# A hybrid layer with a mixture of experts and a two-layer decoder on one core: 36 instead of 40 tokens in the second set of gathered rows, eight row dots moved ahead, and the first loads in quarters

## What is computed

```python
    def per_chunk(args):
        xc, ec, gc = args
        u = expert_u[ec]
        a = jnp.einsum('cd,chkd->chk', xc, u).astype(jnp.float32)
        w = (jax.nn.gelu(a) * gc).astype(xc.dtype)
        return jnp.einsum('chk,chkd->cd', w, expert_v[ec])
```

## Time and profile before

| | |
|---|---|
| median of 3 runs | 1807.74 us (1807.58 to 1809.18) |
| the profiled execution | 1809.13 us |
| its span in the trace | 1807.3 us |
| mean granted clock of TensorE | 0.988 |
| PE busy | 1750.7 us, 97% of the span |
| DVE busy | 1071.6 us, 59% |
| moved by DMA | 439.59 MB |

### The profile page before, as it was taken

The page is one execution under the profiler, slowest core; times in us unless marked ns, Lnnn a source line. Parts: engine busy times, 40 slices in busy tenths (PEclk is TensorE's granted clock), DMA queues, the critical chain, the costliest instruction groups (busy, mean ns, idle before and its releaser), DMA issues.

```text
span 1807.3 us, 29102 instructions
## 1 busy us (share of the span) xinstructions
PE 1750.7 (97%) x11633; PEld 1491.7 (83%) x11633; DVE 1071.6 (59%) x2312; ACT 252.3 (14%) x598; POOL 292.4 (16%) x282
## 2 busy tenths in 40 slices
PE   8999999999999999999999499999999999999996
PEld 7888566986999999999999367699955978699942
DVE  2851432589855886998433743259974223369964
ACT  1004530111443111000000011111100001111100
POOL 0010000033333342444332500000000000000000
PEclk9999999999999999999999699999999999999998
DMA  7535224378999999999999953364554434354551
GB/s 278 190 138 165 93 94 140 125 280 296 418 417 415 408 387 383 364 414 415 416 418 417 373 211 121 131 238 164 167 184 163 162 118 168 126 173 166 173 175 47
DMA packets 76463, 439.59 MB, mean 243 GB/s; under 512 B 8562, under 2 KB 8640, under 8 KB 37568
## 3 DMA queue, kind: packets, MB, share of 16 engines
q1 hardware_dynamic: 42336, 304.11, 45.6%
q0 software_dynamic: 32592, 126.44, 18.1%
q10 hardware_dynamic: 1424, 7.47, 1.0%
HBM read 432.67 MB, written 5.24 MB: 242 GB/s over the span
## 4 chain that ended last, share of the span: by engine, by line
PE 86%; DMA 8%; DVE 3%; issue 1%; ACT 1%; POOL 0%; DVEq 0%; POOLq 0%; ACTq 0%
PE ps L864 15%; PE ps L1104 12%; PE ps L498 10%; PE ps L540 9%; PE ps L456 9%; PE ps L872 6%; DMA arena<-v_rows,sparse_pairs 6%; PE ps L1125 4%; PE ps L578 3%; DMA arena<-u_rows,sparse_pairs 2%; PE ps L732 2%; PE ps L779 2%; PE ps L842 2%; PE ps L745 1%; DVE arena L1945 1%; PE ps L959 1%
## 5 line engine op out<-in xcount | busy, mean ns | idle before, releaser
L872 PE MATMUL ps<-arena,ring 128*128 128x152 f32 (+1 forms) x2048 | 269.7, 293 | 0.4 <-DMA ring<-stream 0.4
L864 PE MATMUL ps<-xT,ring 128*128 128x152 f32 x2048 | 269.7, 293 | 0.0
L872 PEld LDWEIGHTS ps<-arena,ring 128*128 128x128 f32 x2048 | 265.5, 190 | 1.1 <-issue 1.1
L864 PEld LDWEIGHTS ps<-xT,ring 128*128 128x128 f32 x2048 | 265.7, 190 | 0.5 <-issue 0.5
L498 PE MATMUL ps<-ring,arena 128*128 128x512 f32 x416 | 181.4, 592 | 0.4 <-ACT arena L1406 0.4
L1945 DVE SCALAR_TENSOR_TENSOR arena<-arena,sparse_dots 128x1024 f32<-128x1024 f32 x105 | 134.7, 1283 | 76.1 <-DMA arena<-v_rows,sparse_pairs 70.5
L540 PEld LDWEIGHTS ps<-xT,ring 128*128 128x128 f32 x1536 | 173.4, 192 | 3.0 <-issue 2.9
L540 PE MATMUL ps<-xT,ring 128*128 128x128 f32 x1536 | 174.1, 275 | 0.0
L1831 DVE CUSTOM_DVE_ANT_0 arena<-arena 128x1024 f32<-128x1024 f32 x107 | 128.2, 1222 | 68.8 <-DMA arena<-u_rows,sparse_pairs 68.2
L2371 POOL DMA_INDIRECT arena<-u_rows,sparse_pairs x107 | 126.0, 1177 | 213.4 <-DVE sparse_dots L1831 183.6
L2371 POOL DMA_INDIRECT arena<-v_rows,sparse_pairs x107 | 129.5, 1211 | 185.0 <-DVE arena L1945 123.8
(11 more groups left out here) (329 smaller groups left out, 2162.1 us busy)
## 6 DMA issues: line engine op xcount, KB each, us to landing
ring<-stream SPq DMA_DIRECT2D x288, 1024.0 KB, 6.7
arena<-second_params POOLq DMA_DIRECT2D x6, 1024.0 KB, 5.5
arena<-kv_scratch POOLq DMA_DIRECT2D x2, 2048.0 KB, 14.3
kv_scratch<-arena POOLq DMA_DIRECT2D x2, 1024.0 KB, 6.6
kv_scratch<-arena ACTq DMA_DIRECT2D x2, 1024.0 KB, 10.7
arena<-held_params ACTq DMA_DIRECT2D x1, 2048.0 KB, 16.5
arena<-u_rows,sparse_pairs POOLq DMA_INDIRECT x107, 13.1
arena<-v_rows,sparse_pairs POOLq DMA_INDIRECT x107, 13.7
```

The lines of the kernel that those rows point to most:

```text
L864: ins = pe.matmul(ps[:, o % 2, 0:DENSE], w[:, (o % 2) * D + k * P:(o % 2) * D + (k + 1) * P], xT[:, k, 0:DENSE], start=(k == 0), stop=(k = ...
L872: ins = pe.matmul(ps[:, 4 + k // 2, c:c + DENSE], w[:, (o % 2) * D + k * P:(o % 2) * D + (k + 1) * P], H[:, n, :], start=False, stop=last, ...
```

## The change

The second set of tokens by rows has 36 instead of 40 tokens, so 100 of 256 go by rows and `DENSE` is 156. The dense tokens then make 20 gate groups of 8, of which the last has 4 tokens. `DOTS_HEAD` goes from 2 to 4, `DOTS_ROUTING` from 38 to 46, `DOTS_FIRST` from 56 to 60. `SETS_B`, `PAIRS_B`, `CHUNKS`, `U_FIRST`, `ROWS` and the 48 adds of the second mixed stage stay. Both first loads are issued as four quarters instead of two halves.

```diff
-SPARSE_B = 40
+SPARSE_B = 36
 SETS_B = P // SPARSE_B
 SPARSE = SPARSE_A + SPARSE_B
 DENSE = T - SPARSE
 GROUP = 8
-GROUPS = DENSE // GROUP
+GROUPS = -(-DENSE // GROUP)
 PAIRS_HALF = 64
 PAIRS_B = -(-P // SETS_B)
 CHUNKS = PAIRS_HALF + PAIRS_B
 PH_LATE = 4
-DOTS_HEAD = 2
+DOTS_HEAD = 4
 DOTS_EARLY = DOTS_HEAD * PH_LATE
-DOTS_ROUTING = 38
-DOTS_FIRST = 56
+DOTS_ROUTING = 46
+DOTS_FIRST = 60
...
-            half = SLOT // 2
-            sp.dma_start(ring[:, 0, 0:half], streams[0][0][:, 0:half]).then_inc(first_half_in, 16)
-            sp.dma_start(ring[:, 0, half:], streams[0][0][:, half:]).then_inc(loaded[0], 16)
+            quarter = SLOT // 4
+            for n in range(3):
+                c = slice(quarter * n, quarter * (n + 1))
+                sp.dma_start(ring[:, 0, c], streams[0][0][:, c]).then_inc(first_quarter_in[n], 16)
+            sp.dma_start(ring[:, 0, 3 * quarter:], streams[0][0][:, 3 * quarter:]).then_inc(loaded[0], 16)
...
-            pe.wait_ge(first_half_in, 16)
-            pe.wait_ge(mem_half_in, 16)
             for k in range(KT):
-                if k == KT // 2:
+                if k == 6:
                     pe.wait_ge(mem_in, 16)
                     slot("k0", 0)
+                elif k % 2 == 0:
+                    pe.wait_ge(first_quarter_in[k // 2], 16)
+                    pe.wait_ge(mem_quarter_in[k // 2], 16)
...
-            half = KT * T // 2
-            act.dma_start(mem_raw[:, 0:half], mem_d[:, 0:half]).then_inc(mem_half_in, 16)
-            act.dma_start(mem_raw[:, half:], mem_d[:, half:]).then_inc(mem_in, 16)
+            quarter = KT * T // 4
+            for n in range(3):
+                c = slice(quarter * n, quarter * (n + 1))
+                act.dma_start(mem_raw[:, c], mem_d[:, c]).then_inc(mem_quarter_in[n], 16)
+            act.dma_start(mem_raw[:, 3 * quarter:], mem_d[:, 3 * quarter:]).then_inc(mem_in, 16)
...
-                w = min(P, DENSE - i * P)
+                w = min(P, GROUPS * GROUP - i * P)
...
-                h = H[:, hf * HALF_BLOCKS:(hf + 1) * HALF_BLOCKS, g * GROUP:(g + 1) * GROUP]
-                dve.scalar_tensor_tensor(h, h, 1.0 / GSCALE, ps[:, 2 + b, :].rearrange("p (t n) -> p n t", t=GROUP),
+                n = min(GROUP, DENSE - g * GROUP)
+                h = H[:, hf * HALF_BLOCKS:(hf + 1) * HALF_BLOCKS, g * GROUP:g * GROUP + n]
+                dve.scalar_tensor_tensor(h, h, 1.0 / GSCALE, ps[:, 2 + b, :].rearrange("p (t n) -> p n t", t=GROUP)[:, :, 0:n],
                                          ALU.mult, ALU.mult).then_inc(gates_applied, 1)
```

More of the change, by code:

```diff
@@ L173, in build @@
         mark_cell = sb("mark_cell", [P, 1])
-        sel16 = sb("sel16", [P, 4, DENSE], F16)
+        sel16 = sb("sel16", [P, 4, GROUPS * GROUP], F16)
         e1 = sb("e1", [P, 2, 2, GROUP, HEAD], F16)
@@ L387, in build @@
         xkv_ready, xq_ready = sem("xkv_ready"), sem("xq_ready")
-        first_half_in, mem_half_in = sem("first_half_in"), sem("mem_half_in")
+        first_quarter_in = [sem(f"first_quarter_in_{n}") for n in range(3)]
+        mem_quarter_in = [sem(f"mem_quarter_in_{n}") for n in range(3)]
         mem_in, kv_spilled, kv_in = sem("mem_in"), sem("kv_spilled"), sem("kv_in")
```

## The result

| | before | after |
|---|---|---|
| median of 7 runs | 1808.11 us (1807.00 to 1809.18) | 1813.24 us (1812.62 to 1814.09) |
| ratio, 95% interval | | 1.003 (1.0021 to 1.0039) |
| the profiled execution, its span | 1809.13, 1807.3 us | 1812.62, 1810.8 us |

The change costs 5.1 us, where +5.4 us was forecast.

A forecast was written before the change was run, and what follows sets the result against it. PE's passes set the time, except one wait for the row path, bound after 740 us by DMA bytes shared with the stream. +6.9 - 1.5 = +5.4 us on 1807.74 gave 1813.1 us; range over the cases 1809.5 to 1817.0.

The forecast's parts named there:

- The tokens, +6.9: End of the row path: add 91 comes +6.6 us later, or +7.3 reckoned by bytes; +6.9 taken.
- The start of the second mixed stage: DVE's L1986 waits for ACT's gelu after PE's last up-block, so it moves with PE's passes: +7.3 us.
- PE's last wait: PE's wait at L959 for the row path shrinks from 24 to about 16 us and stays.
- ten less 5.8 gathers: Last row adds: 7.3 us more of full rate before the stream stops fetches 5.8 gathers earlier, 8.0 us.
- 0 to 1.3 us: Second mixed stage: gathers may fall behind the DMA engines by at most one gather, 1.3 us; 0 taken.
- The second rival: Row path: gathers stay at 3.2 us each while the stream runs; +9.9 us, 1817.6 us; chance 0.10.
- The early dots, 0: Eight dots moved into tile 1's routing: DVE about 11 us later there, hidden by waits; the lead is lost later.
- a net lead of four gathers: First mixed stage: eight dots ahead, four more to do; some 13 us less waiting, DVE done near 558 us.
- the cover: DVE's slack before the gates, done near 558 us, needed at 574.76 plus 3.4; without it PE waits microsecond for microsecond.
- The first rival: End of the row path: the eight-gather lead lives on to add 91, 11 us off, about 1802 us; chance 0.05.
- The first loads, -1.5: PE's start: the first quarter lands near 5.4 us instead of 6.95, gain kept; bounds 0 and -3.1 us.
- the 1.6 us added behind the bytes: First loads: delay from bytes moved to the landing PE saw, added to 3.85 us for a quarter.

The follow-up runs named there:

- e2: Kernel before with only 36 instead of 40 tokens in set B (20 gate groups), loads in halves, dots not moved; 1815.41 us, ratio 1.0043.
- e3: Kernel before with only the dots moved ahead (4 per head, 46, 60), 40 tokens, loads in halves; 1809.11 us, ratio 1.0006.
- e7: Kernel of e3 with ACT's exponentials of tile 0's gates after 28 instead of 24 up-blocks; 1808.02 us, ratio 1.0001 to the kernel before.
- e8: Changed kernel with four PE matmuls on a zero tile ahead of the first loads' wait; 1813.52 us, ratio 1.0032 to the kernel before.
- e5: Changed kernel with `U_FIRST` 103 instead of 96, seven more dots ahead of the v rows; 1803.18 us, ratio 0.9974 to the kernel before.
- e1: Kernel before with only the first loads in quarters instead of halves; 1805.78 us, ratio 0.9988.
- e6: Kernel of e5 with 42 tokens in set B, `U_FIRST` 107 and exponentials after 28 up-blocks; 1787.78 us, ratio 0.989 to the kernel before.
- e4: Kernel before with 42 instead of 40 tokens in set B (150 dense columns); 1806.60 us, ratio 0.999.

## Why the prediction was right

**The tokens, +6.9.** Measured alone +7.5 (e2; interval 5.2 to 10.1). The steps: a pass of 156 columns was put at 129.3 + 3.3 = 132.6 ns and took 132.5. The start of the second mixed stage was put 7.3 us later through PE's passes; U to M grew by 7.15 us in both kernels with 36 tokens. PE's last wait was put at 16 us and was 17.4 (17.1 in e2). Fewer than ten adds back to back were forecast, ten less 5.8 gathers or about four, and there were six. PE's work from its first up-block to its last wait grew by 13.9 us, where 14.6 was put, and PE's start behind that wait came 588.38 us after the first up-block instead of 580.94, +7.4 us (e2: +7.1). One reading would explain two more adds: the last stage moved 412 GB/s and not 416, 4 GB/s less over 264 us, 1.06 MB, two gathers. That is an account from two windows, not an experiment; if it holds, the 0 taken out of "0 to 1.3 us" for the gathers falling behind was too low.

**The rates add up.** The first and the last dot of the eleven late u rows, before and after, stood at

```profile
906.08 1.23 DVE L1831 CUSTOM_DVE_ANT_0 arena<-arena 128x1024 f32<-128x1024 f32 x1 [2.20 <-DMA arena<-u_rows,sparse_pairs]
...
938.46 1.23 DVE L1831 CUSTOM_DVE_ANT_0 arena<-arena 128x1024 f32<-128x1024 f32 x1 [2.21 <-DMA arena<-u_rows,sparse_pairs]
```

```profile
907.18 1.23 DVE L1837 CUSTOM_DVE_ANT_0 arena<-arena 128x1024 f32<-128x1024 f32 x1 [1.55 <-DMA arena<-u_rows,sparse_pairs]
...
938.29 1.23 DVE L1837 CUSTOM_DVE_ANT_0 arena<-arena 128x1024 f32<-128x1024 f32 x1 [1.60 <-DMA arena<-u_rows,sparse_pairs]
```

Ten intervals in each: 3.24 us a gather before, 3.11 after. A slot of the stream is 32 passes, 4.14 us before and 4.24 after, or 253 and 247 GB/s; what is left of 416, the rate from 880 to 935 us in both traces, is 163 and 169, 3.22 and 3.10 us for 0.524 MB. So the gathers do get what the slower stream leaves. The second rival, with gathers that keep their 3.2 us, has fallen, and its +9.9 us lies outside the measured interval (3.8 to 7.1). The trace agrees with the rule of the Trainium skill (DMA: Bandwidth & Descriptors, SWDGE vs HWDGE vs iDMA) named there, by which each engine takes its queues in turn; it does not show how the engines choose.

**The early dots, 0.** The end was right: U to M of the changed kernel equals e2's, and e3 shows no gain. The steps to it were not. DVE was to be done near 558 us, 13 us sooner, by a net lead of four gathers; measured were 565.5 instead of 571, and of these 5.5 us, 2.7 are PE's earlier start of the whole stage and 2.8 have their like in e2 (2.7), without the early dots. The working took eight dots of lead, but at PE's first up-block four were left, and the four more dots use them up. The cost was not nothing either. With 40 tokens the early dots cost 1.6 us of U to M, through ACT's exponentials (e3, e7); in the changed kernel's trace that cost was missed by 0.24 us, and e8's trace has 0.8 us of it. The prediction had looked for the cover at the end of DVE's routing, not at what ACT takes from inside it. So the 0 in the trace after is partly luck. The first rival needed more than 103 gathers fetched at L1986, and the order with its seven buffers forbade it; e5 shows a gain as soon as the order puts more of them ahead.

**The first loads, -1.5.** This is the term that was mis-sized: alone they are worth -2.1 us by the medians (e1, interval 0.4 to 3.8). The landing was put at 5.4 us and came at 4.85 (4.81 in e1); the step that failed is the 1.6 us added behind the bytes, taken from a half, since from 3.85 us on it was only 1.0. The quarters landed 3.96 us after their issue, the halves of before 6.1 us, a difference of 2.1 us, and the means over nine traces keep it to the next group of passes, as shown at e1. The fit of the Trainium skill (DMA: Bandwidth & Descriptors, Anatomy of one DMA — SWDGE (gpsimd) path) gives estimates of 3.2 and 4.4 us, short of both and of their difference (1.2 us); the page has it for DMAs issued from GpSimd, and these loads are issued by SP and ACT. The Trainium skill's advice to batch (DMA: Bandwidth & Descriptors, Bandwidth) is about the share of the peak rate; here the time to the first landing counted, and quarters were 2.1 us faster (e1).

**The sum.** +6.9 - 1.5 = +5.4, measured +5.1. By the medians of e2 and e1 both terms were too small by 0.6 us, with opposite signs, and in the sum that cancels; the intervals of both runs are too wide to make more of it. The three parts alone give +7.5 - 2.1 + 1.2 = +6.6 us; their intervals are 1.6 to 2.5 us wide to each side, so this does not differ from +5.1.

The two spans differ by 3.5 us, and the traces say where. PE's first group took 9.82 instead of 8.70 us, so the 2.10 us of the earlier start are 0.98 at L459. The 160 passes that follow the short ones near 100 us took 34.62 us in the changed kernel and, in before,

```profile
102.03 36.31 PE ps L456 x160
```

so 1.69 us are less in the changed kernel. From the first up-block to PE's start behind its last wait it is 7.44 us more, and from there to the end of the span 1.25 less (784.40 and 785.65 us). -0.98 - 1.69 + 7.44 - 1.25 is +3.5. The second term is the clock's. Granted clock and PE's busy time in before and then in the changed kernel:

```profile
100.00:108.00 8.00, 8.00 (x40) 6.98 (x40) 4.61 (x8) 0.21 (x1) 3.11 (x2) 0.79 0.05 19
```

```profile
100.00:108.00 8.00, 8.00 (x43) 7.17 (x43) 4.62 (x7) 0.21 (x1) 3.11 (x2) 1.00 0.01 3
```

In the ten traces of this study the group took 34.62 us four times (the changed kernel, e2, e6, e7), 36.31 five times (before, e1, e3, e4, e5) and 37.57 once (e8). With the halves, the quarters, 40 or 36 tokens both of the first two lengths occur, so it is no effect of the change. The last stretch, too, scatters from 784.4 to 785.7 us without an order that the changes explain. Which of these terms the medians have, no trace shows; the +5.1 rests on the seven executions of each kernel.

**What neither rival nor forecast said:** that the DMA engines had room in the first mixed stage was in the rows (387, 383 and 364 GB/s in the three slices from 633 us on the earlier trace rows, 393 and 289 in the earlier trace rows), and using it was worth more than anything in the change: 10 us with seven dots (e5), and 20 us below before with all of them, 42 tokens and quarters together (e6).

## What to carry to other kernels

A stream and a gather that share the DMA engines share one sum (here 412 to 416 GB/s), so work taken off a stage's DMA is only worth something if what remains is fetched there; find the stages whose sum is below it (here 364 and 300) and change the order of fetching so that they fill, before shifting work between two paths. Work done ahead in a fixed order is worth nothing at a point that the order lets no further work pass: ask at each such point how much of the lead the order and the buffers can hold (here 96 dots and 7 rows). A wait that grows along with a change of two things need not come from the one that suggests itself: here the kernel with only the other one had the same wait (8.9 and 9.0 us). And when an engine's work is delayed, look not only at the end of its block but at each result in it that another engine takes (ACT's exponentials in e3 and e8), for the waiting engine stands in order and carries the delay to a third.

## What the runs showed of the hardware

Two traces are compared at places behind it, by a distance that begins behind it, as U to M here, which came out the same to 0.01 us over three kernels (before, e1, e7) and again over two (the changed kernel, e2).
